# Sample latent attention: half of the cached pages read from a second, already turned host layout

## The reference

```python
def page_step(carry, pt):                      # pt: page number of each sequence
    lat = lat_pool[e, pt]                      # (8, 128 tokens, 256)
    kr = rope_pool[e, pt]                      # (8, 128 tokens, 32)
    s = (einsum('bhqc,bkc->bhqk', q_lat, lat) + einsum('bhqr,bkr->bhqk', q_rope, kr)) * MLA_SCALE
    m_new = maximum(m, max(s)); p = exp(s - m_new)
    acc = acc * exp(m - m_new) + einsum('bhqk,bkc->bhqc', p, lat)
```

## Time and profile before

| | us |
|---|---|
| median of the runs | 1580.4 |
| the profiled execution, whole | 1582.64 |
| its span, first to last instruction | 1580.9 |
| the stage, TensorE's first to the first output matmul | 601.0 to 707.1 |

### The profile page before, as it was taken

One profiled execution on the slowest core, in us unless ns is written; L12 is line 12 of the kernel. 1 busy time (PEld: TensorE's weight loads), 2 busy tenths in 40 slices (PEclk: granted clock), 3 DMA queues, 4 the chain that ended last, 5 costly groups with the idle time before them and its releaser, 6 DMA issues.

```text
span 1580.9 us, 24315 instructions
## 1 busy us (share of the span) xinstructions
PE 1476.9 (93%) x10022; PEld 1298.7 (82%) x10022; DVE 784.7 (50%) x1444; ACT 577.5 (37%) x1030; POOL 38.2 (2%) x68
## 2 busy tenths in 40 slices
PE   5999999999999888889998999999999999999993
PEld 5988999866666565559997798999999989989992
DVE  3475643164554554555784143324444358526674
ACT  3057312144545554342453123204444115212343
POOL 1000000000000000000000100000000001000000
PEclk9999999999999999999998999999999899999997
DMA  5110032220001061735554230120011121114552
GB/s 198 42 40 28 28 108 94 74 82 13 1 1 54 1 185 49 203 124 167 168 191 165 94 107 28 49 52 27 28 30 57 70 81 41 42 39 149 170 190 73
DMA packets 51920, 132.13 MB, mean 84 GB/s; under 512 B 6601, under 2 KB 30394, under 8 KB 51042
## 3 DMA queue, kind: packets, MB, share of 16 engines
q1 hardware_dynamic: 46114, 111.45, 22.6%
q0 software_dynamic: 5696, 19.12, 3.3%
HBM read 117.08 MB, written 13.47 MB: 83 GB/s over the span
## 4 chain that ended last, share of the span: by engine, by line
PE 53%; DVE 3%; issue 2%; ACT 2%; POOL 0%; DVEq 0%; POOLq 0%; ACTq 0%
PE ps L538 9%; PE ps L540 9%; PE ps L539 9%; PE ps L592 4%; PE ps L593 4%; PE ps L594 4%; PE ps L1620 2%; PE ps L2051 1%; PE ps L1129 1%; PE ps L1645 1%; DVE ln_sq L769 1%; PE ps L2243 1%; PE ps L1917 1%; PE ps L1373 1%; PE ps L1915 1%
## 5 line engine op out<-in xcount | busy, mean ns | idle before, releaser
L538 PE MATMUL ps<-x_hi,w_hi 128*128 128x352 f32 x1416 | 472.8, 334 | 22.5 <-DVE w_lo L488 20.0
L540 PE MATMUL ps<-x_hi,w_lo 128*128 128x352 f32 x1416 | 458.6, 324 | 0.0
L539 PE MATMUL ps<-x_lo,w_hi 128*128 128x352 f32 x1416 | 458.1, 324 | 0.0
L538 PEld LDWEIGHTS ps<-x_hi,w_hi 128*128 128x128 f32 x1416 | 269.2, 190 | 32.0 <-DVE w_lo L488 20.3
L539 PEld LDWEIGHTS ps<-x_lo,w_hi 128*128 128x128 f32 x1416 | 270.0, 191 | 2.5 <-issue 1.2
L540 PEld LDWEIGHTS ps<-x_hi,w_lo 128*128 128x128 f32 x1416 | 268.8, 190 | 0.0
L482 ACT ACTIVATE w_hi<-w_raw 128x1024 fp32r<-128x1024 f32 (+1 forms) x107 | 123.3, 1152 | 311.0 <-PE ps L540 201.9
L488 DVE TENSOR_TENSOR w_lo<-w_raw,w_hi 128x1024 fp32r<-128x1024 f32 (+1 forms) x107 | 143.5, 1341 | 64.6 <-ACT w_hi L482 64.0
L592 PE MATMUL ps<-mx_hi,w_hi 128*128 128x352 f32 x480 | 158.1, 329 | 1.5 <-DVE mx_lo L679 1.2
L594 PE MATMUL ps<-mx_hi,w_lo 128*128 128x352 f32 x480 | 154.4, 322 | 0.0
L593 PE MATMUL ps<-mx_lo,w_hi 128*128 128x352 f32 x480 | 154.4, 322 | 0.0
(11 more groups left out here) (456 smaller groups left out, 1887.7 us busy)
## 6 DMA issues: line engine op xcount, KB each, us to landing
w_raw<-in_w_out SPq DMA_DIRECT2D x48, 640.0 KB, 3.9
w_raw<-in_w_in SPq DMA_DIRECT2D x59, 512.0 KB, 3.6
page<-in_cache_mla SPq DMA_DIRECT2D x128, 144.0 KB, 2.6
kvs<-in_mem_cache SPq DMA_DIRECT2D x16, 512.0 KB, 6.0
x_res<-in_xT SPq DMA_DIRECT2D x24, 176.0 KB, 2.4
x<-x_next POOLq DMA_DIRECT2D x3, 1408.0 KB, 8.1
x_res<-x SPq DMA_DIRECT2D x24, 176.0 KB, 2.3
out_y<-res POOLq DMA_DIRECT2D x3, 1408.0 KB, 5.9
```

Of the source, the lines that this page charges most:

```text
L538: pe.matmul(out, w_hi[:, u % 2, kk], x_hi[:, k, chunk(c)], start=(k == 0), stop=False)
L539: pe.matmul(out, w_hi[:, u % 2, kk], x_lo[:, k, chunk(c)], start=False, stop=False)
L540: mm = pe.matmul(out, w_lo[:, u % 2, kk], x_hi[:, k, chunk(c)], start=False, stop=(k == KX - 1))
```

## The change

The host hands over the latents without the rotated channels (cache_mla), once more with the channels in rows (cache_lT: 128 rows of two times 128 tokens), and the rotated channels turned (cache_rope: 32 rows of 128 tokens). Of the four pages q = 0 to 3 of a sequence in a step, pages 0 and 1 also come from cache_lT by DMA; only pages 2 and 3 are still turned by TensorE. So turn has four units of four transposes in place of nine units, and latT is half as wide. The rotated channels of all pages come by 16 DMAs a step on GpSimd's queue into one of three ropeT buffers. Scores start with the rotated channels, go on with the turned pages, and wait for the units only before the second half.

SP's queue issues 24 DMAs a step in place of 16. In front of r = 2 it waits for `ms_done` and not for `ms_o`; behind r = 7 it waits for scores(8) (`ss_z` 9), since turned0 lies in w_raw. The split of the first output weight tile moves from e == 8 to e == 9, since turned2 lies in w_hi. Buffers, the new load code, and the scores:

```diff
         cursor[0] = X0
-        page01 = keep("page", [P, 2, 4, 4, 288])
-        latT = keep("latT", [P, 4, 2, 512])
-        ropeT = keep("ropeT", [P, 512])
+        page01 = keep("page", [P, 2, 4, 4, LAT])
+        turned1 = keep("turned1", [P, 4, 2, 2, P])
+        assert cursor[0] <= at["vh"]
+        latT = keep("latT", [P, 4, 2, 256])
-        page2 = place("page2", [P, 4, 4, 288], Z0 + 10 * ROWS)
+        page2 = place("page2", [P, 4, 4, LAT], Z0 + 10 * ROWS)
+        turned0 = place("turned0", [P, 4, 2, 2, P], W0)
+        ropeT = [place("ropeT0", [P, 512], at["turned0"]), place("ropeT1", [P, 512], at["page2"]),
+                 place("ropeT2", [P, 512], at["page2"] + 2048)]
+        turned2 = [place("turned2a", [P, 2, 2, 2, P], S0), place("turned2b", [P, 2, 2, 2, P], S0 + 10240)]
         pages = [page01[:, 0], page01[:, 1], page2[:, :]]
...
-                    if w == 8:
-                        for q in range(4):
-                            for j in range(4):
-                                mm = pe.matmul(ps[32 * j:32 * j + 32, b, q * P:q * P + P],
-                                               pages[r % 3][:, q, j, LAT:LAT + ROPE], ident[:, :],
-                                               start=True, stop=True)
-                    else:
-                        for q in range(2):
-                            for k in range(2):
-                                mm = pe.transpose(ps[:, b, (2 * k + q) * P:(2 * k + q + 1) * P],
-                                                  pages[r % 3][:, 2 * (w % 2) + q, w // 2, k * P:k * P + P],
-                                                  ident[:, :])
+                    for q in range(2):
+                        for k in range(2):
+                            mm = pe.transpose(ps[:, b, (2 * k + q) * P:(2 * k + q + 1) * P],
+                                              pages[r % 3][:, 2 + q, j, k * P:k * P + P],
...
-                    pe.wait_ge(pgT_ev[par], (9 * (real(e) + 1) + 1 - par) // 2)
-                for k in range(2):
-                    for j in range(4):
-                        pe.matmul(ps[32 * j:32 * j + 32, e % 2, :], rows_of(qs[:, k], g, j), latT[:, j, k, :],
-                                  start=(k == 0), stop=False, skip_group_check=True)
+                pe.wait_ge(rp_in[real(e) % 3], 256 * (real(e) // 3 + 1))
                 for j in range(4):
                     rr = slice(32 * j, 32 * j + 32)
-                    mm = pe.matmul(ps[rr, e % 2, :], rows_of(qsr[rr], g, j), ropeT[rr, :], start=False, stop=True,
-                                   skip_group_check=True)
+                    pe.matmul(ps[rr, e % 2, :], rows_of(qsr[rr], g, j), ropeT[real(e) % 3][rr, :], start=True,
+                              stop=False, skip_group_check=True)
+                for part in range(2):
+                    if part:
+                        for par in range(2):
+                            pe.wait_ge(pgT_ev[par], 2 * (real(e) + 1))
+                    for k in range(2):
+                        for j in range(4):
+                            keys = latT[:, j, k, :] if part else turned(real(e), j)[:, :, k, :]
+                            mm = pe.matmul(ps[32 * j:32 * j + 32, e % 2, 256 * part:256 * part + 256],
+                                           rows_of(qs[:, k], g, j), keys, start=False, stop=(k == 1),
+                                           skip_group_check=True)
                 mm.then_inc(ss_z, 1)
 
...
-                if e == 8:
+                if e == 9:
                     act_hi(act, W_OUT[0])
...
-                if e == 8:
+                if e == 9:
                     dve_lo(dve, W_OUT[0])
...
                     numbers.append(four)
                 if r == 2:
-                    sp.wait_ge(ms_o, 1)
-                    sp.dma_start(w_uv[:, :, :, :], x["w_uv"]).then_inc(smp_in, 16)
+                    sp.wait_ge(ms_done, 8)
+                    sp.dma_start(w_uv[:, :, :, :], x["w_uv"]).then_inc(tbl_in, 16)
                 elif r >= 3:
                     sp.wait_ge(ss_o, 5 * ((r - 3) // 4) + 2 + (r - 3) % 4)
                 for j in range(4):
-                    for q in range(4):
+                    for q in (2, 3, 0, 1):
                         sp.dma_start(pages[r % 3][:, q, j, :],
                                      x["cache_mla"][bass.ds(numbers[j][q], 1), :, :].rearrange(
                                          "a p c -> (a p) c")).then_inc(pg_in[r % 3][j // 2], 16)
+                    for q in range(2):
+                        sp.dma_start(turned(r, j)[:, q, :, :].rearrange("p k n -> p (k n)"),
+                                     x["cache_lT"][bass.ds(numbers[j][q], 1), :, :].rearrange(
+                                         "a p c -> (a p) c")).then_inc(pg_in[r % 3][j // 2], 16)
+            sp.wait_ge(ss_z, 9)
             sp_steps(sp, 0)
             for u in range(W_IN1, W_OUT[1]):
                 if u == 72:
@@ -2572,6 +2579,20 @@
             n_out[0] += 16
             gp.wait_ge(kr_ready, 1)
             gp.dma_start(o["kr"], z[0:32, Z_KR, :]).then_inc(z_out, 16)
+            gp.wait_ge(tbl_in, 32)
+            gp.wait_ge(o_ready, len(PAIRS))
+            for r in range(8):
+                if r >= 3:
+                    gp.wait_ge(ss_o, 5 * ((r - 3) // 4) + 2 + (r - 3) % 4)
+                for j in range(4):
+                    n = (4 * (r // 4) + j) * NPG + 4 * (r % 4)
+                    _, four = nc.values_load_multi_w_load_instructions(
+                        table[0:1, n:n + 4], engines=[mybir.EngineType.Pool], min_val=0, max_val=NPHYS - 1,
+                        skip_runtime_bounds_check_because="a page table holds numbers of pages")
+                    for q in range(4):
+                        gp.dma_start(ropeT[r % 3][32 * j:32 * j + 32, q * P:q * P + P],
+                                     x["cache_rope"][bass.ds(four[q], 1), :, :].rearrange(
+                                         "a c p -> (a c) p")).then_inc(rp_in[r % 3], 16)
             for c in range(NCH):
                 gp.wait_ge(ln_y, KX * (c + 1))
                 gp.dma_start(x1d[:, :, chunk(c)], x_next[:, :, chunk(c)]).then_inc(spill, 16)
...
     a["lru_h0"] = i["state_lru_h"][0].T.reshape(4, P, NB).transpose(1, 0, 2)
     a["lru_c0"] = i["state_lru_conv"][0].transpose(2, 0, 1).reshape(4, P, NB, 3).transpose(1, 0, 2, 3)
-    a["cache_mla"] = np.concatenate([i["cache_mla_latent"][0], i["cache_mla_krope"][0]], axis=2)
+    a["cache_mla"] = i["cache_mla_latent"][0]
+    a["cache_lT"] = a["cache_mla"].reshape(NPHYS, PAGE, 2, P).transpose(0, 3, 2, 1).reshape(NPHYS, P, 2 * PAGE)
+    a["cache_rope"] = i["cache_mla_krope"][0].transpose(0, 2, 1)
     a["page_table"] = i["page_table"].reshape(1, NB * NPG)
 
     a["mem_cache"] = np.stack([i["cache_mem_k"].reshape(2, NB, NMEM, 2, P).transpose(0, 1, 4, 3, 2),
```

More of the change, by code:

```diff
@@ L409, in build @@
         pgT_ev = [sem("pgT_ev_a"), sem("pgT_ev_v")]
-        smp_in = sem("smp_in")
+        rp_in = [sem(f"rp_in{c}") for c in range(3)]
         l96_in = sem("l96_in")
@@ L1580, in build, with turned @@
         UNIT_BANKS = (2, 3, 6)
+        def turned(r, j):
+            return (turned0, turned1)[r % 3][:, j] if r % 3 < 2 else turned2[j // 2][:, j % 2]
         def real(e):
@@ L1586, in unit_out @@
         def unit_out(n):
-            r, w = n // 9, n % 9
-            if w == 8:
-                return ropeT[:, :]
-            return latT[:, w // 2, :, 256 * (w % 2):256 * (w % 2) + 256]
+            return latT[:, n % 4, :, :]
         def unit_in(n):
-            b = bank(UNIT_BANKS[n % 3])
-            return b if n % 9 == 8 else b.rearrange("p (k c) -> p k c", k=2)
+            return bank(UNIT_BANKS[n % 3]).rearrange("p (k c) -> p k c", k=2)
         def pe_mla_sample(pe):
@@ L1603, in turn @@
                 r = real(e)
[L1604 to L1607, removed]
+                for j in range(4):
+                    n = 4 * r + j
+                    if j in (0, 2):
+                        pe.wait_ge(pg_in[r % 3][j // 2], 192 * (r // 3 + 1))
                     if n >= 3:
@@ L1610, in turn @@
                     b = UNIT_BANKS[n % 3]
-                    if w == 8:
-                        for q in range(4):
-                            for j in range(4):
-                                mm = pe.matmul(ps[32 * j:32 * j + 32, b, q * P:q * P + P],
-                                               pages[r % 3][:, q, j, LAT:LAT + ROPE], ident[:, :],
-                                               start=True, stop=True)
-                    else:
-                        for q in range(2):
-                            for k in range(2):
-                                mm = pe.transpose(ps[:, b, (2 * k + q) * P:(2 * k + q + 1) * P],
-                                                  pages[r % 3][:, 2 * (w % 2) + q, w // 2, k * P:k * P + P],
-                                                  ident[:, :])
+                    for q in range(2):
```

(25 more changed lines are left out.)

## The result

| | before | after |
|---|---|---|
| median of 8 runs, us | 1580.4 (1579.4 to 1582.2) | 1587.6 (1584.7 to 1590.1) |
| profiled execution, whole / span | 1582.64 / 1580.9 | 1587.67 / 1586.1 |
| stage: TensorE's first self scores to the first output matmul | 603.23 to 707.08 = 103.85 | 600.79 to 709.34 = 108.55 |

After over before is 1.0044, with a 95% interval of [1.0033, 1.0055]: slower by 7.0 us (5.2 to 8.7). The forecast was 1585.0, in a range of 1578 to 1594, with slower as the likeliest; in the stage it was +4.6 us, and the traces show +4.7. The other 2.5 us of the 7.2 between the medians were not forecast.

A forecast was written before the change was run, and what follows sets the result against it. SP's page DMA issues would replace TensorE as the stage's bound: 619.4 + 71.8 + 2.6 + 4.5 + 1.6 + 11.8 put the first output matmul at 711.7, +4.6 us, so 1585.0 us against the 1580.4 median; range 1578 to 1594.

The forecast's parts named there:

- The bound: In the stage, TensorE's step falls from 10.5 to 7.5 us, but SP's page DMA issues need 14.7 us a group.
- SP's queue: Page DMAs: 24 issues at 0.56 us plus 1.3 us make 14.7 us a group; no waits after r = 3.
- The landing: After the last page DMA's issue at 691.2 us, its page lands 2.6 us later, at 693.8.
- the train: SP's last five groups run without a wait: 119 pitches of 0.56 plus four gaps of 1.3, 71.8 us; chance 0.76.
- The last stretch: From the end of the last scores to the first output matmul: 10.6 us before, 11.8 forecast, ending at 711.7.
- The moved w_lo: The output weight split, now ahead of the reciprocal on VectorE, delays the path by 1.5 us, net +1.2.
- an earlier mx_lo: On VectorE, mx_lo(9) no longer stands behind w_lo and starts some 0.3 us earlier, reducing +1.5 to +1.2.
- the price of the low clock: TensorE's idling drops its clock to 1.2 GHz; 1.6 us added once, at the last step.
- Behind 711.7 nothing changes: From the first output matmul, forecast at 711.7 us, to the end, the kernel takes no more time than before.
- GpSimd's queue: Rotated channels: 16 DMAs at 0.55 us plus 1.3 make 10.1 us a step, hidden under SP's 14.7.
- Rival C: In the stage, bytes bind, not the queue: 10.7 us a step at 318 GB/s; -13.7 us, 1566.7; chance 0.12 with other fast cases.
- Rival B: GpSimd's queue for rotated channels becomes the bound at 1.02 us a DMA: +16.4 us, 1596.8; chance 0.12.

The follow-up runs named there:

- tiny: Changed kernel with four more unused 1 KiB DMAs per group on SP's queue, one ahead of each sequence; 1597.83 us, ratio 1.0119 to the kernel before.
- pool_small: Changed kernel with four more small unused DMAs per group on GpSimd's queue; 1588.41 us, ratio 1.0052 to the kernel before.
- merged: w_lo_back with latents and turned latents side by side, so SP issues 16 DMAs a step, not 24, for the same bytes; 1570.95 us, ratio 0.9941.
- w_lo_back: Changed kernel with the split of the first output weight (w_lo) moved back behind the scaling of the result; 1585.56 us, ratio 1.0035 to the kernel before.
- warm: w_lo_back with 36 unneeded transposes of ident ahead of TensorE's last wait for a page; 1582.88 us, ratio 1.0012 to the kernel before.
- rope_only: Kernel before with only the rotated channels moved to GpSimd's queue, all latents still turned by TensorE; 1573.60 us, ratio 0.9956.
- rope_four: rope_only with four ropeT buffers in place of three, each freed by the scores that read it; 1572.18 us, ratio 0.9946 to the kernel before.
- rope_warm: rope_four with 26 unneeded transposes of ident in the four gaps behind the last scores; 1570.71 us, ratio 0.9932 to the kernel before.
- rope_four_again: rope_four unchanged, run again beside rope_warm on the same chip; 1573.19 us, ratio 0.9953 to the kernel before.

## Why the prediction was right

**The bound.** As forecast, TensorE's work stopped counting and SP's issues set the stage: tiny, pool_small and merged show it from three sides. The working, term by term, from the start of the stage (603.23 before):

| step | predicted | measured |
|---|---|---|
| stage's start to r = 3 on SP | 619.4 - 603.23 = 16.2 | 616.37 - 600.79 = 15.6 |
| to the last page DMA | 71.8 | 687.0 - 616.37 = 70.6 |
| to TensorE's last units | 2.6 | 690.45 - 687.0 = 3.45 |
| units, probabilities, scores | 4.5 + 1.6 = 6.1 | 695.63 + 1.05 - 690.45 = 6.2 |
| to the first output matmul | 11.8 | 709.34 - 696.68 = 12.7 |
| sum | 108.5 | 108.55 |

**SP's queue** was right in price (14.7 us a group against 14.6 to 15.1) and in that it never waits again. The landing was 0.85 us longer than the median row, and the last stretch 0.9 longer; the train was 1.2 and its start 0.6 shorter. The errors cancel, so +4.7 against +4.6 is partly luck. So is 1585.0 against 1587.6: 2.5 us of the loss lie outside the stage, where the forecast had nothing (below).

**The last stretch** was sized too small in two ways. The moved w_lo was given +1.2; the gap shows +1.4 (2.88 against 1.45), and w_lo_back takes just that away. The 0.3 us that an earlier mx_lo was to give back did not come: the gap ahead of the first output matmul is 1.24 us in both kernels. And the price of the low clock was taken once, for the scores. It came again in the transposes and the value projection behind the next idle time: 0.69 + 1.91 us in place of 0.44 + 1.13, another 1.0, and warm shows both parts by removing them, 2.7 us together (1.9 from the last units to the end of the scores, where 1.6 was forecast, and 0.7 in the value projection). The wait for the last probabilities was some 0.3 shorter, which leaves the 0.9. "Behind 711.7 nothing changes" was wrong as well: the first forty output matmuls took 0.9 us more, at the lower clock for longer. The earlier trace rows had shown the same fall of the clock behind an idle stretch; the step to take was to look for every short idle time that follows, not the next one alone. The Trainium skill (TensorE: Matmul & The Clock Gate, HAM oscillation — how this bites in real kernels) describes waits for DMA after which work starts at the lower clock each time, and advises, among other things, to restructure the loop so that TensorE stays warm; the traces agree (granted clock 0.52, 0.50 and 0.56 in the windows from 660, 675 and 690 on, each behind such a wait), and warm does it without restructuring.

**GpSimd's queue**: 16 x 0.55 + 1.3 = 10.1 us a group forecast, 10.6 measured (four times 2.22 us for four DMAs and 0.43 us for the load of their numbers). Hidden, as forecast.

**Rival C** (bytes) falls for this kernel. The condition given for it, a pitch under 0.45 us, left out the 1.3 us between groups; with them 24 issues fit into 10.7 us only at 0.39. With 16 issues in place of 24 the bytes may begin to count: in merged the DMA engines are full (share 0.99 and 1.02). No run here moves fewer bytes with merged's issues, so that is not shown. **Rival B** (GpSimd) falls with pool_small, and no score matmul waited for ropeT in the changed kernel. The Trainium skill's rule (DMA: Bandwidth & Descriptors, Issuing engines are not separate DMA queues) that the time to initiate a DMA is usually small beside the DMA holds here for one DMA alone and not for a train. The issue takes 0.52 us against 2.6 to 2.9 from issue to landing; but the landings overlap and the issues of one queue do not, and 131 KB at the 313 GB/s of merged's window are 0.42 us.

**What was not forecast** is the part of the loss outside the stage. Of +7.2 us in the medians the stage has 4.7. The slower first output matmuls have 0.9 and the end of the span 1.0, each of them in both traces of both kernels. About 0.5 isn't assigned: that is inside the interval (5.2 to 8.7 us), and the start of the stage moves by up to 2 us between two executions of one program. The two profiled executions differ by only 5.0 us (1582.64 and 1587.67), since the one before lay 2.2 over its median and the one after on it. The cause of the longer end is open. It isn't the number of DMAs on GpSimd's queue alone: rope_only and rope_four have the same 128 and end 12.7 and 13.9 us behind the last store. Nor is it the number of semaphores in the program: tiny, rope_only, rope_four and pool_small each have three more than the kernel before and end at 12.6, 12.7, 13.9 and 14.95. What does go with it is how many different semaphores the DMAs added to GpSimd's queue raise: none before (11.6), three in the changed kernel, tiny and rope_only (12.6 to 12.7), four in rope_four (13.9) and pool_small (14.95, with 32 DMAs more). No run varied that number alone.

## To carry to other kernels

Price a queue by its pitch from issue to issue and not by the duration of one, and compare count times pitch with what the other engines need for a step: here 16 issues were just hidden and 24 were not, whatever TensorE saved. Where a second layout is wanted, lay it beside the first so that one DMA brings both, or send it by a queue with nothing to do. When TensorE starts to idle, charge the lower clock behind every gap, and in the first microseconds of the next long stretch of work too. Four versions beat both kernels (merged, rope_only, rope_four, rope_warm: 0.993 to 0.996 of the time before), and their intervals don't tell them apart. Spreading the page DMAs over ScalarE's queue as well was not tried.

## What the runs showed of the hardware

- The clock fell behind short gaps that no DMA ended: in rope_four TensorE had gaps of 0.99, 1.46, 0.47 and 1.23 us behind its last scores, still with 1.00 granted from 685 to 690, and then had 0.52 from 690 to 695. In warm the value projection at 704.37 still had the full clock and the output matmuls at 706.74 not.
- With the DMA engines full a page takes longer to land: in merged a median of 3.7 us for the 128 KB pages and 4.1 for the 256 KB ones, against 2.6 and 2.9 for the two kinds of 128 KB in the changed kernel.
- On GpSimd's queue an address from a register does not lengthen the DMA's own record (0.497 us for 32 rows of 512 bytes, 0.503 for pool_small's 16 rows of 64 bytes with a fixed one), but it widens the distance between two: sixteen with fixed addresses in the kernel before start 0.493 us apart (868.12 to 875.51), and four with addresses from registers take 2.22 us in the changed kernel, which is (2.22 - 0.50)/3 = 0.575. So it costs 0.08 us, where the forecast added 0.05, from SP's queue.

```profile
868.12 0.51 POOL L2584 DMA_DIRECT2D g_i<-gates  x1 [1.88 <-DMA gates<-mx]
...
875.51 0.50 POOL L2586 DMA_DIRECT2D g_f<-gates  x1
```
```profile
559.49 2.22 POOL L2593 DMA_DIRECT2D ropeT<-in_cache_rope  x4 [0.43 <-issue]
```

- The end of the span, behind the last store, is fixed for a kernel within 0.05 us and takes four values 1.0 to 1.3 us apart over these kernels (11.6, 12.7, 13.9, 14.95).
- The clock at the start of the stage differs between executions of one program: the first 32 transposes took 4.25 us in rope_four (granted clock 1.00 from 600 to 605) and 5.38 in rope_four_again (0.70).
